# Attention output with features on partitions, its normalising factors spread by TensorE

## The reference

```python
for i in range(2):
    if i == 0: mix = moba_attention(h, moba_w_qkv, moba_w_o, cos, sin)       # 16 heads
    else:      mix = dilated_attention(h, dil_w_qkv, dil_w_o, cos, sin)      # 12 heads
    h = layer_norm(ALPHA * h + mix, ...)
    h = layer_norm(ALPHA * h + sq_relu_mlp(h, ...), ...)
```

```python
p = exp(s - lse);  o_g = p @ v                      # for each group g of 4 heads
alpha = softmax(stack([lse_0, lse_1, lse_2]), axis=0)
o = concat(o_g * alpha_g) @ w_o
```

## Time and profile before

| | us |
|---|---|
| median of three runs | 1373.94 (1371.58 to 1374.4) |
| the profiled execution, its own time | 1369.73 |
| its span in the trace | 1367.9 |
| PE busy over the span | 1200.8 (88%) |
| DVE busy, ACT busy | 647.3 (47%), 485.5 (35%) |

### The profile page before, as it was taken

One profiled execution on the slowest core, in us unless ns is written; L12 is line 12 of the kernel. 1 busy time (PEld: TensorE's weight loads), 2 busy tenths in 40 slices (PEclk: granted clock), 3 DMA queues, 4 the chain that ended last, 5 costly groups with the idle time before them and its releaser, 6 DMA issues.

```text
span 1367.9 us, 22195 instructions
## 1 busy us (share of the span) xinstructions
PE 1200.8 (88%) x9439; PEld 924.5 (68%) x9439; DVE 647.3 (47%) x982; ACT 485.5 (35%) x695; POOL 0.2 (0%) x4
## 2 busy tenths in 40 slices
PE   5999999999867665766766899999999999999997
PEld 4677688887434333433433599878888799888886
DVE  4445336786121010210201377576666767766665
ACT  5552346565001000000000346454444456554443
POOL 0000000000000000000000000000000000000000
PEclk9999999999998887997887999999999999999999
DMA  9657666569999999999999972436364544554620
GB/s 343 256 193 249 217 226 245 209 236 395 427 418 428 429 428 427 426 428 428 428 428 427 399 270 89 158 123 243 130 243 145 180 155 155 185 202 168 221 88 31
DMA packets 89115, 371.95 MB, mean 272 GB/s; under 512 B 6490, under 2 KB 8328, under 8 KB 76364
## 3 DMA queue, kind: packets, MB, share of 16 engines
q1 hardware_dynamic: 87480, 369.73, 68.9%
q10 hardware_dynamic: 1556, 1.08, 0.3%
HBM read 369.74 MB, written 1.05 MB: 271 GB/s over the span
## 4 chain that ended last, share of the span: by engine, by line
PE 71%; DMA 22%; DVE 3%; ACT 2%; issue 1%; SPq 1%; ACTq 0%; DVEq 0%
DMA arena<-in_moe_w 20%; PE ring L2011 8%; PE ring L2452 7%; PE ring L2000 5%; PE acc L2099 4%; PE acc L2100 4%; PE acc L2101 4%; PE ring L2013 4%; PE ring L2002 2%; PE acc L1984 2%; PE acc L1985 2%; PE acc L1986 2%; PE ring L2145 1%; PE ring L2147 1%; PE ring L2146 1%
## 5 line engine op out<-in xcount | busy, mean ns | idle before, releaser
L2452 PE MATMUL ring<-arena 128*32 128x256 f32 x2048 | 153.7, 466 | 74.9 <-DMA arena<-in_moe_w 74.9
L2452 PEld LDWEIGHTS ring<-arena 128*32 128x32 f32 x2048 | 78.9, 133 | 145.1 <-issue 73.5
L1273 DVE TENSOR_TENSOR wlo<-arena,whi 128x2048 fp32r<-128x2048 f32 x56 | 128.0, 2290 | 49.9 <-ACT whi L832 49.9
L1681 DVE TENSOR_TENSOR arena<-arena,ring 128x128 f32<-128x128 f32 x32 | 12.1, 379 | 258.8 <-ACT arena L1077 258.8
L1077 ACT ACTIVATE arena<-ring 128x128 f32<-128x128 f32 x32 | 8.9, 277 | 349.1 <-PE ring L2452 349.1
L832 ACT ACTIVATE whi<-arena 128x2048 fp32r<-128x2048 f32 x56 | 106.8, 1910 | 42.2 <-PE acc L2101 25.5
L2011 PE MATMUL ring<-xboth,whi 128*128 128x512 f32 x320 | 113.8, 399 | 0.0
L2013 PE MATMUL ring<-xboth,wlo 128*128 128x256 f32 x320 | 90.0, 281 | 0.0
L2471 PE MATMUL ring<-arena 128*32 128x256 f32 x1024 | 61.9, 382 | 29.6 <-DVE arena L1684 28.8
L2471 PEld LDWEIGHTS ring<-arena 128*32 128x32 f32 x1024 | 31.7, 110 | 57.9 <-DVE arena L1684 31.8
L2011 PEld LDWEIGHTS ring<-xboth,whi 128*128 128x128 f32 x320 | 60.2, 188 | 14.6
(11 more groups left out here) (413 smaller groups left out, 2655.1 us busy)
## 6 DMA issues: line engine op xcount, KB each, us to landing
arena<-in_moe_w SPq DMA_DIRECT2D x94, 2048.0 KB, 21.0
arena<-in_mlp_w_in SPq DMA_DIRECT2D x16, 2048.0 KB, 10.5
arena<-in_mlp_w_out SPq DMA_DIRECT2D x16, 2048.0 KB, 7.6
arena<-in_w_mod SPq DMA_DIRECT2D x11, 2048.0 KB, 8.5
arena<-in_w_in SPq DMA_DIRECT2D x11, 2048.0 KB, 9.2
arena<-in_moba_w_qkv SPq DMA_DIRECT2D x6, 2048.0 KB, 19.0
arena<-in_dil_w_qkv SPq DMA_DIRECT2D x4, 2048.0 KB, 8.9
arena<-in_w_gla_br SPq DMA_DIRECT2D x2, 2048.0 KB, 7.7
```

The source lines that it names most:

```text
L1273: dve.tensor_tensor(lo, raw, hi.bitcast(F32), ALU.subtract).then_inc(G["split_ready"], 1)
L2452: ins = pe.matmul(o, xs[:, kt, j, :], w[kt][g], start=(kt == 0), stop=(kt == KT - 1))
```

## The change

`weighted` takes the values as the stationary side and moves the turned exponentials: the output of a head then has its 64 features on partitions and 256 tokens in columns. Even heads of a group go to partitions 0 to 63, odd heads to partitions 64 to 127. It is one matmul with 256 columns and one with 128, where there were three with 64.

`crossed` and its transposes go. The factor of a token can no longer be applied as a number for each partition, so `factors(g)` makes PE spread it: for each head and each half of the tokens, a matmul whose stationary side is the column `share[:, tt, h]` repeated 64 times, and whose moving side is the identity, gives a 64x128 block with the factors of the tokens in every row. That is eight fp32 matmuls for a group, into the bank that `crossed` used. ACT now copies the output of every group to `att` (`unscaled`), DVE multiplies `att` by the bank of factors (`scaled`), and `high` and `low` read `att` in SBUF.

On PE `factors(g)` stands one step earlier than `crossed` did in layer 0 (behind step 3 of the k product; behind piece 8 instead of 10 for group 3), and waits for the reciprocals (`share_ready`). In layer 1 `factors(2)` stands ahead of the first piece of the output projection.

```diff
                 def unscaled(g):
                     act.wait_ge(G["weighted_done"], groups_before(l, g) + 1)
-                    act.activation(att[:, g, :, :], output_bank(l).rearrange("p (a n) -> p a n", a=TT), ACT.Copy).then_inc(G["att_ready"], 1)
+                    if l == 0 and g >= 3:
+                        act.wait_ge(G["attlo_ready"], g - 2)
+                    act.activation(att[:, g % 3, :, :], output_bank(l).rearrange("p (k t) -> p k t", k=2), ACT.Copy).then_inc(G["att_ready"], 1)
 
                 def high(g):
-                    act.wait_ge(G["crossed_done"], groups_before(l, g) + 1)
-                    b = cross_bank(l, g).rearrange("p (k t) -> p k t", k=2)
-                    act.activation(atthi[:, 2 * g:2 * g + 2, :], b, ACT.Copy).then_inc(G["atthi_ready"], 1)
+                    act.wait_ge(G["scaled_ready"], groups_before(l, g) + 1)
+                    act.activation(atthi[:, 2 * g:2 * g + 2, :], att[:, g % 3, :, :], ACT.Copy).then_inc(G["atthi_ready"], 1)
...
-                def normalised(g):
+                def scaled(g):
+                    dve.wait_ge(G["att_ready"], groups_before(l, g) + 1)
+                    dve.wait_ge(G["factor_ready"], groups_before(l, g) + 1)
+                    v = att[:, g % 3, :, :]
+                    dve.tensor_tensor(v, v, factor_bank(l, g).rearrange("p (k t) -> p k t", k=2), ALU.mult).then_inc(G["scaled_ready"], 1)
+
+                def shares(g):
                     f = share[:, :, GROUP * g:GROUP * g + GROUP]
                     dve.wait_ge(G["exp_ready"], heads_before(l, g) + GROUP)
-                    link(dve.reciprocal(f, ssum[:, :, GROUP * g:GROUP * g + GROUP]))
-                    dve.wait_ge(G["weighted_done"], groups_before(l, g) + 1)
-                    scaled(g, output_heads(), f)
+                    dve.reciprocal(f, ssum[:, :, GROUP * g:GROUP * g + GROUP]).then_inc(G["share_ready"], 1)
...
                     hv = slice(HD * j, HD * j + HD)
-                    o = [b[:, 256 * tt + HD * j:256 * tt + HD * j + HD] for tt in range(TT)]
-                    pe.matmul(o[0], p_[:, 0:P], vt[:, g % 2, 0, hv], start=True, stop=True)
-                    pe.matmul(o[1], p_[:, P:2 * P], vt[:, g % 2, 0, hv], start=True, stop=False)
-                    ins = pe.matmul(o[1], p_[:, 2 * P:3 * P], vt[:, g % 2, 1, hv], start=False, stop=True)
+                    o = output_bank(l)[HD * (j % 2):HD * (j % 2) + HD, T * (j // 2):T * (j // 2) + T]
+                    pe.matmul(o, vt[:, g % 2, 0, hv], p_[:, 0:2 * P], start=True, stop=False, skip_group_check=True)
+                    ins = pe.matmul(o[:, P:T], vt[:, g % 2, 1, hv], p_[:, 2 * P:3 * P], start=False, stop=True, skip_group_check=True)
                     if j == GROUP - 1:
                         ins.then_inc(G["weighted_done"], 1)
 
-                def crossed(g):
-                    pe.wait_ge(G["scaled_ready"], groups_before(l, g) + 1)
-                    b = cross_bank(l, g)
-                    for j in range(2):
+                def factors(g):
+                    pe.wait_ge(G["share_ready"], g + 1 if l == 0 else GROUPS[0] + 1)
+                    b = factor_bank(l, g)
+                    for j in range(GROUP):
+                        p_, o = slice(HD * (j % 2), HD * (j % 2) + HD), T * (j // 2)
                         for tt in range(TT):
-                            ins = pe.transpose(b[:, j * T + tt * P:j * T + (tt + 1) * P], att[:, g % 3, tt, j * P:(j + 1) * P], ident)
-                    ins.then_inc(G["crossed_done"], 1)
+                            h = GROUP * g + j
+                            ins = pe.matmul(b[p_, o + tt * P:o + (tt + 1) * P], share[:, tt, h:h + 1].to_broadcast([P, HD]), ident, start=True, stop=True)
+                    ins.then_inc(G["factor_ready"], 1)
```

More of the change, by code:

```diff
@@ L361, in build @@
         by_sin = at(35 * K1 + 512, 2, T)
-        att = at(34 * K1, 3, TT, GROUP * HD)
+        att = at(34 * K1, 3, 2, T)
         vt = at(36 * K1, 2, TT, GROUP * HD)
@@ L1857, in _ @@
                     split_lo(h1_ + 2)
-                    normalised(3)
+                    shares(3)
+                    scaled(3)
                     split_lo(h1_ + 3)
@@ L1897, in _ @@
                     link(dve.reciprocal(total[:, :, :], total[:, :, :]))
[L1898 to L1901, removed]
+                    dve.tensor_tensor(grouped(f12), grouped(f12), over_groups(total[:, :, :]), ALU.mult).then_inc(G["share_ready"], 1)
+                    scaled(0)
+                    scaled(1)
                     low(0)
                     low(1)
-                    dve.wait_ge(G["weighted_done"], groups_before(1, 2) + 1)
-                    scaled(2, output_heads(), share[:, :, 2 * GROUP:3 * GROUP])
+                    scaled(2)
                     split_lo(h1_ + 1)
                     low(2)
+                    dve.wait_ge(G["attlo_ready"], groups_before(1, 3))
                     split_lo(h1_ + 2)
@@ L2634, in _ @@
                                     weighted(g - 1, kt + 2)
-                                if kt == 4:
-                                    crossed(g - 1)
+                                if kt == 3:
+                                    factors(g - 1)
                             if kind == "v" and kt == 6:
@@ L2646, in _ @@
                             weighted(3, n - 4)
-                        if n == 10:
-                            crossed(3)
+                        if n == 8:
+                            factors(3)
                     for k in range(2):
@@ L2673, in _ @@
                         pe.wait_ge(G["pT_ready"], heads_before(1, 2) + 2 + g)
-                        crossed(g)
+                        factors(g)
                     for j in range(GROUP):
@@ L2678, in _ @@
                     product_read(pe, 1, 8)
+                    pe.wait_ge(G["pT_ready"], heads_before(1, 3))
+                    factors(2)
                     for k in range(2):
                         proj_step(0, 0, k)
-                    crossed(2)
+                    pe.wait_ge(G["att_ready"], groups_before(1, 2) + 1)
                     for g, tt in ((0, 1), (1, 0), (2, 0), (1, 1)):
```

26 lines of the change are left out of this document (11 added, 15 removed).

## The result

| | before | after |
|---|---|---|
| median of six runs each | 1372.76 us | 1381.88 us (1380.7 to 1384.46) |
| ratio to before, 95% interval | | 1.0069 (1.0057 to 1.0081) |
| the profiled execution | 1369.73 us | 1381.35 us |
| attention of layer 0, by the trace | 109.1 us | 116.9 us |
| attention of layer 1, by the trace | 93.1 us | 95.5 us |

The change makes the kernel 0.69% slower, about 9.5 us. Forecast were 12.5.

The account below looks back on a forecast made before the run. PE was taken as the bound in attention: lone heads +7.4, lone factors +4.9, layer 1's block +0.4, a vanished wait -0.2, together +12.5 us on 1373.9, giving 1386.4 us; 70% for 1383 to 1390, wider range 1380 to 1393.

Parts of the forecast that it names:

- PE is the bound, so the cost is the sum on PE's list: Both attention stretches: PE busy nearly without a gap, so its own added time is the cost, +12.5 us together.
- A lone head 0.98 us: 24 heads alone between projection steps: 0.98 us each against 0.67, +0.31 each, +7.4 us together.
- An excursion 0.34 us: PE's way from full-array matmuls into the 64-column shape and back: 0.34 us lost each time, 0.42 as upper value.
- the change of shape is free: Rival: entering and leaving the 64-column shape costs PE nothing in attention; +0.9 us, 1374.8 us in all; chance 9%.
- 64 columns run as part of the full shape: Rival: the new matmuls are not half-width, so no shape change and no pairing; +7.5 us, 1381.4 us; chance 5%.
- Factors 1.07 us of streaming: Five lone groups of factors: neighbours in different halves pair, 1.07 us plus 0.34 less 0.44, +0.97 each, +4.9 us.
- The block in layer 1: Factors of two groups, then four heads, in one shape: 4.41 us after against 3.96 before, +0.4 us.
- the last factors: Last group of layer 1, counted among five lone places of factors, with 0.34 us for the shape change: +0.97 us.
- The wait for `attlo` goes: End of layer 0, group 3: PE no longer stands waiting for `attlo`, -0.2 us.
- The slower rival: Rival: in attention no matmuls pair and each shape change costs 0.42 us; +20.3 us, 1394.2 us; chance 13%.
- The fastest rival: Rival: in attention the array's halves run side by side, two heads sharing it; -5.4 us, 1368.5 us; chance 3%.
- What costs nothing: ACT's and DVE's added work in attention is covered; tightest is layer 0's group 3, holding by 0.2 us.

Follow-up runs that it names:

- e5: The changed kernel with every matmul of the factors issued twice, the same results written again; 1388.9 us, ratio 1.0116 to the kernel before.
- e2: The changed kernel with 128 stationary columns in each head matmul instead of 64, part of the results wrong; 1376.56 us, ratio 1.0027 to the kernel before.
- e1: The changed kernel with a group's four heads issued in a row instead of singly between projection steps; 1371.38 us, ratio 0.9989 to the kernel before.
- e3: On top of e1, heads of each group in the order 0, 2, 1, 3; 1373.66 us, ratio 1.0004 to the kernel before.
- e4: The changed kernel with a group's heads issued in two pairs instead of singly between projection steps; 1371.97 us, ratio 0.9993 to the kernel before.
- e7: On top of e1, layer 0's factors follow the four heads directly, no projection step between; 1368.03 us, ratio 0.9972 to the kernel before.
- e8: On top of e1, layer 0's factors are written wide by DVE and transposed by PE; 1368.51 us, ratio 0.9966 to the kernel before.

## Why the prediction was right or wrong, point by point

- **PE is the bound, so the cost is the sum on PE's list.** Right: the feed-forward between is unchanged to 0.1 us, and a doubled piece of that list (e5) came out at its full price.
- **A lone head 0.98 us, 24 times +0.31.** Right: 1.22 us between the steps, as forecast to the hundredth. e2 shows the cause: the same matmuls in the full width cost 0.66.
- **An excursion 0.34 us.** Right for lone heads. Around a group's factors it is 0.40 (e5), and around four heads in a row too (e1). The rivals that the change of shape is free, and that 64 columns run as part of the full shape, fall by the same rows. e2 agrees with the rule of the Trainium skill ("TensorEngine Tiling (Array Packing)", section Key Properties) that a change of tiling mode drains TensorE: it shows the price, 0.32 us. That the price is a drain no run here shows.
- **Factors 1.07 us of streaming.** This term of the sum was mis-sized. I let only a matmul and its very next neighbour in the other half pair. They all paired, 0.87 us, because a matmul also pairs with one two places ahead of it (e1, e3). In the four places of layer 0 that gives +0.83 each instead of +0.97, 0.6 us too much.
- **The block in layer 1 and the last factors.** I had +0.4 for the block and +0.97 for the last factors, 1.4 us; from 0.34 + 3 x 0.90 + 1.30 = 4.34 against 3.96 + 0.44 = 4.40 before, it is -0.1. Three errors. Two are the same as above: heads paired completely, 1.30 where my slots gave 1.93, and factors took 0.90, not 1.07. The third is another one: I charged the last factors a way in and out of their own (0.34), though they stand directly behind the four heads, in the same shape. 1.5 us too much.
- **The wait for `attlo` goes.** Right, 0.2 us. But in layer 0 7.8 us are measured where heads and factors alone give 16 x 0.31 + 4 x 0.83 = 8.3. The rest is the second wait that went, at 885.12 in the trace before, about 0.26 us. My sum had no term for it: I had priced a head by those that cost 0.67 and did not look at the one that costs 0.93.
- Together: 12.5 - 0.6 - 1.5 - 0.2 = 10.2, which is what the trace shows. The time, 1381.88 us, lies within the range from 1380 to 1393, but below the 1383 to 1390 to which I gave 70%: the errors listed here all made the forecast too high, and 1.2 us more come from the base, 1373.9 by three runs and 1372.76 by six. The total alone would not have told my account from the rival that the matmuls are not half-width at all, which came to 1381.4; the rows do, by the shape 128*64, the 1.22 us and the pairs. The slower rival (nothing pairs) failed on its main condition.
- **The fastest rival**, that halves run side by side, was refused for the right reason, where the heads stand alone. e1 and e4 are its test: as soon as two heads of different halves stand together, the second is free. The gain by the advice of the Trainium skill on the swap ("TensorEngine Tiling (Array Packing)", section Performance Considerations) is real here, 1.30 us for four heads against 2.68 (1.70 with the way in and out), and the changed kernel does not collect it for six of its seven groups because of where they stand in PE's order.
- **What costs nothing.** Held in the changed kernel: PE's rows name no new wait. The tightest place, `attlo` of group 3, was ready at 900.21 (899.53 + 0.68), and PE came to its piece at 900.77, so it held by 0.56 us, not 0.2. It stops holding in e1, e7 and e8, where PE stands 0.6 us for DVE at the end of layer 0, and in e1, e4, e7 and e8, where the weight loads of three transposes of layer 0 stand 0.2 us each for ACT.

## What to carry to other kernels

Price a small matmul by what it does to the distance of the large ones around it, and count changes of array shape as instructions of their own, 0.34 to 0.40 us for a way in and out here. A change to half-width matmuls pays only if they are also gathered, so that the halves pair and one way in and out serves many. Before paying with PE for spreading a number over partitions, ask whether an engine with time left can write it wide and PE merely transpose it (0.44 us against 1.27).

## What the runs showed of the hardware that I had not expected

- Two halves of the array overlap over more than the next matmul. In e1 the list is L2585, L2586, L2585, L2586, and the records start as four of L2585, then four of L2586: the second head's first matmul starts beside the first head's first, which is two places ahead of it in the list, and so ahead of the first head's second. In e3, where four matmuls of one half stand ahead of the other half's first, the first two run alone: nothing started beside a matmul four places ahead. So by these traces matmuls of different halves do not start in the order of the list.
- A run of several pairs costs a little more on the way in and out (0.40 us around factors and around four heads) than one head or one pair (0.34, 0.35). In e1 the extra 0.05 us lies within the first pair, which takes 0.70 us (815.33 to 816.03) instead of 0.65; why is open.
